# Products of the matrix of ones at seven places of TensorE's program, in an encoder of two layers

## What is computed

```
for l in range(DEPTH):                       # DEPTH = 2
    u = rms_norm(h, attn_norm_w[l])
    (dn_q, ..., ml_kr) = split_columns(u @ w_in[l])
    y_dn = gated_deltanet(...)               # 4 heads, both directions, chunked
    y_df = diff_attention(...)               # 4 heads, two softmaxes each
    y_ml = mla_attention(...)                # 4 heads, latent q and kv, rotary key
    h = h + concatenate([y_dn, y_df, y_ml]) @ w_out[l]
    u = rms_norm(h, ffn_norm_w[l])
    if l % 2 == 0: h = h + swiglu(u, w_gate, w_up, w_down)
    else:          h = h + moe_swiglu(u, router_w, ...)   # top 2 of 8 experts
return h[:, N_META:]
```

## Time and profile before

| | |
|---|---|
| median of 3 runs | 1974.53 us (1974.48 to 1975.61) |
| the profiled execution | 1975.23 us, its span 1973.4 us |
| mean granted clock of TensorE | 0.979 of full speed |
| busy: PE / DVE / ACT / POOL | 96% / 75% / 57% / 6% of the span |
| the chain that ended last | PE 88%, DVE 10%, issue 2% |
| HBM | 224 GB/s over the span |
| in-projection, first layer | about 10 to 128 us |
| mixers, first layer | 130 to 330 us |
| out-projection, feed-forward, first layer | 330 to 592 us |
| in-projection, second layer | 595 to 711 us |
| mixers, second layer | 713 to 905 us |
| out-projection, router, gather | 905 to 975 us |
| experts | 975 to 1970 us |

### The profile page before, as it was taken

How to read it: one execution, slowest core, us unless ns; L and a number is a source line. 1 busy time by engine, 2 the same in 40 slices (tenths; PEclk the granted TensorE clock), 3 DMA queues, 4 the chain that set the end, 5 groups by cost and what they waited for, 6 DMA issues and landing times.

```text
span 1973.4 us, 27118 instructions
## 1 busy us (share of the span) xinstructions
PE 1902.5 (96%) x10976; PEld 1626.6 (82%) x10976; DVE 1480.8 (75%) x1828; ACT 1125.5 (57%) x1249; POOL 117.7 (6%) x107
## 2 busy tenths in 40 slices
PE   9998989899999979999999999999999999999998
PEld 8987768899998967779888888888888888888886
DVE  8659666655549566756688888989889788888986
ACT  5644424433334633424677777677777777777775
POOL 1004131000000004140000000000000000000000
PEclk9998989999999998999899999999999999999999
DMA  7500001544453200005599999989999899999994
GB/s 298 177 28 1 1 1 68 200 171 171 155 182 134 97 28 1 1 3 180 191 364 345 353 352 366 352 333 353 358 360 347 340 358 351 358 356 364 356 361 178
DMA packets 64195, 443.56 MB, mean 225 GB/s; under 512 B 8172, under 2 KB 8204, under 8 KB 13632
## 3 DMA queue, kind: packets, MB, share of 16 engines
q1 hardware_dynamic: 62032, 437.87, 59.2%
q0 software_dynamic: 1760, 3.78, 0.5%
q10 hardware_dynamic: 272, 0.10, 0.0%
HBM read 440.66 MB, written 2.17 MB: 224 GB/s over the span
## 4 chain that ended last, share of the span: by engine, by line
PE 88%; DVE 10%; issue 2%; ACT 0%; DMA 0%; POOL 0%; SPq 0%; DVEq 0%; POOLq 0%; ACTq 0%
PE ps L1916 23%; PE ps L1918 23%; PE ps L1917 23%; PE ps L2311 2%; PE ps L2296 2%; PE ps L2315 2%; PE ps L1929 2%; DVE w_lo L1186 2%; DVE cacc L1278 2%; PE ps L2490 1%; PE ps L2090 1%; PE ps L2501 1%; PE ps L2137 1%; PE ps L2173 1%; PE ps L2102 0%
## 5 line engine op out<-in xcount | busy, mean ns | idle before, releaser
L1243 DVE TENSOR_TENSOR m_lo<-raw,m_hi 128x2048 fp32r<-128x2048 f32 x336 | 768.3, 2289 | 135.9 <-ACT m_hi L839 135.7
L839 ACT ACTIVATE m_hi<-raw 128x2048 fp32r<-128x2048 f32 x336 | 644.1, 1918 | 269.1 <-PE ps L1918 269.0
L1916 PE MATMUL ps<-m_hi,xe_hi 128*128 128x512 f32 x896 | 358.6, 400 | 0.0
L1918 PE MATMUL ps<-m_lo,xe_hi 128*128 128x512 f32 x896 | 353.6, 395 | 0.0
L1917 PE MATMUL ps<-m_hi,xe_lo 128*128 128x512 f32 x896 | 353.6, 395 | 0.0
L1186 DVE TENSOR_TENSOR w_lo<-raw,w_hi 128x1024 fp32r<-128x1024 f32 (+1 forms) x164 | 183.2, 1155 | 116.3 <-ACT w_hi L804 116.3
L1916 PE MATMUL ps<-u_hi,w_hi 128*128 128x272 f32 x800 | 236.7, 296 | 14.3 <-DVE u_lo L1236 9.9
L1918 PE MATMUL ps<-u_lo,w_hi 128*128 128x272 f32 x800 | 232.9, 291 | 0.0
L1917 PE MATMUL ps<-u_hi,w_lo 128*128 128x272 f32 x800 | 231.9, 290 | 0.0
L804 ACT ACTIVATE w_hi<-raw 128x1024 fp32r<-128x1024 f32 (+1 forms) x164 | 159.5, 1002 | 116.5 <-PE ps L1918 107.5
L1918 PEld LDWEIGHTS ps<-m_lo,xe_hi 128*128 128x128 f32 x896 | 168.0, 187 | 41.1
(11 more groups left out here) (397 smaller groups left out, 2765.4 us busy)
## 6 DMA issues: line engine op xcount, KB each, us to landing
raw<-in_moe_units SPq DMA_DIRECT2D x336, 1024.0 KB, 4.8
raw<-in_dense_units SPq DMA_DIRECT2D x57, 1024.0 KB, 4.8
raw<-in_dense_units SPq DMA_DIRECT2D x16, 768.0 KB, 5.6
raw<-in_dense_units SPq DMA_DIRECT2D x8, 896.0 KB, 4.5
w_uq<-in_mla_w_uq SPq DMA_DIRECT2D x2, 768.0 KB, 4.6
mats<-in_c_mats POOLq DMA_DIRECT2D x1, 1216.0 KB, 10.5
h<-in_h_rows SPq DMA_DIRECT2D x2, 544.0 KB, 4.4
bias_rows<-bias_row POOLq DMA_DIRECT2D x1, 1088.0 KB, 25.9
```

Source lines behind the costliest of these rows:

```text
L839: nc.scalar.activation(m_hi[k % RING][:, :], raw[:, slot, :], ACT.Copy).then_inc(m_hi_ready, 1)
L1243: V.tensor_tensor(m_lo[k % RING][:, :], raw[:, mslot(k), :], m_hi[k % RING][:, :].bitcast(F32), ALU.subtract).then_inc(m_lo_ready, 1)
L1916: mm(o, w[0], x[0], start=first, stop=False)
L1918: return mm(o, w[0], x[1], start=False, stop=last)
```

## The change

`idle_products` gets a second argument, the PSUM bank. TensorE's program calls it at seven more places. Four are in both layers:

1. behind the last `mixer_sums` of the in-projection: 9 products in bank 6;
2. before the first score of the latent attention, ahead of its two waits, with a wait of its own for `log_taken`: 9 products in bank 4;
3. before the wait for `m_prod` (s=0, d=1): 22 products in bank 4;
4. before the wait for the first level's mask of s=1, d=0, with the wait for `expcols` moved ahead of it: 10 products in bank 0.

Three are in the first layer alone: 20 products before the gate and up streams, 8 before the wait for the last hidden tile, and 11 behind the down projection. That makes 2 x 50 + 39 = 139 products. The other engines' instructions are the same as before.

```diff
-            def idle_products(n):
+            def idle_products(n, bank=6):
 
                 for _ in range(n):
-                    mm(ps[:, 6, 0:P], ones, ones, start=True, stop=True)
+                    mm(ps[:, bank, 0:P], ones, ones, start=True, stop=True)
...
                 for i in range(NORM_JOBS - 2, NORM_JOBS):
                     mixer_sums(i)
+                idle_products(9)
...
                             if t == 0:
+                                pe.wait_ge(log_taken, stat[0])
+                                idle_products(9, 4)
                                 dve_ml.wait(pe, 0, "qrot", H - 1)
                                 pe.wait_ge(rstd_used, norms_before + 3 * H)
...
                         dve_w("cols", s)
                         if d and s == 0:
+                            idle_products(22, 4)
                             dve_w("m_prod")
                         S.mark(mm(ps[:, 2 * d + 1, :], ones, flat(B[d]["TT"]), start=True, stop=True), "beta", s, d)
...
                             if n == 0:
+                                if s and d == 0:
+                                    act_w("expcols", s, d)
+                                    idle_products(10, 0)
                                 dve_w("mask", s, 0, d)
                                 act_w("expcols", s, d)
...
                     n_u[0] += KT
+                    idle_products(20)
                     for j, (gg, gu) in enumerate(zip(plan[l]["gate"], plan[l]["up"])):
...
+                    idle_products(8)
                     pe.wait_ge(hid_ready, 11)
                     residual(plan[l]["down"], (hid_hi, hid_lo), cs, T)
+                    idle_products(11)
```

## The result

The changed kernel takes 1962.76 us (median of its executions) against 1975.26 us of the kernel before, both measured again with more executions; the medians are 12.5 us apart. The ratio of the two sets of executions is 0.9923 with a 95% interval of 0.9903 to 0.9944, some 15 us less (11 to 19). The prediction said 1959.5, in 1956.5 to 1968.5.

What follows compares the result with a forecast made beforehand. PE held 88% of the chain that ended last, with ten half-clock stretches. Gains at A, C, D, E, F, H and I, less 0.2 for ten products, summed to 15.3 us off 1975.2; forecast 1959.5, range 1956.5 to 1968.5.

Steps and rivals of the forecast that it cites:

- two main scenarios: H gone and no twin: 1956.5 to 1962.5 us, chance 0.50; one fall of the pair: 1963 to 1968.5, chance 0.35.
- twin: First layer, rest at about 165 to 169 us: a fall like H ahead of PE-paced steps, losing 6.4 us.
- Price of the products: In the filled rests: 0.25 us a product, mostly covered; each group costs its excess over the wait, 0 to 0.3 us.
- Do they hold the clock: In the filled rests: products of ones raised the clock at the program's start, so they hold it; slower had chance 0.03.
- D, E, F: Half-clock stretches at 380.09, 520.04 and 595.13 us, in streams of 272 columns: give back 1.9, 1.5 and 1.5 us.
- A: Half-clock stretch at 130.92 us, first layer, between L2194 and the second beta product: gives back 1.6 us.
- B and G: Half-clock stretches at 154.81 and 735.08 us, behind beta, where TensorE waits for VectorE and POOL: give back 0.
- H: Half-clock stretch at 752.15 us, second layer, no product in its rest: 6.4 us gained if the fall is missed.
- C: Half-clock stretch at 260.63 us, with L2296 the only long PE work: gives back 1.0 us, between 0 and 1.9.
- I: Half-clock stretch at 834.07 us, PE solid for 3.41 us at half pace: gives back 1.6 us.
- first rival: H stays or its twin appears: one fall loses 6.4 us, 1966, chance 0.35; both 1972, chance 0.07.
- J: Half-clock stretch at 953.53 us, with no product: 0, up to 1.7 us either way.

Runs made afterwards that it cites:

- e7: The changed kernel with products in the remaining mixer and router rests too, and four for ten at s=1 of the second layer; 1956.68 us, ratio 0.9895.
- e3: The changed kernel without the 22 products at the beta step, in both layers; 1967.38 us, ratio 0.9958.
- e6: The changed kernel plus 7 products in the second rest (1.6 us) of the second level of s=0, both layers; 1965.18 us, ratio 0.9948.
- e10: e7 without the 22 products at the beta step, in both layers; 1955.66 us, ratio 0.9879.
- e2: The kernel before with only the 22 products at the beta step added, in both layers; 1973.05 us, ratio 0.9970.
- e11: e7 without the 8 and 7 products in the two rests of the second level of s=0, both layers; 1962.42 us, ratio 0.9919.
- e4: The changed kernel plus 8 products in the first rest (2.2 us) of the second level of s=0, both layers; 1972.92 us, ratio 0.9962.

## Why the prediction was right, and where its steps were off

The time, the sign and the range held. The point was 3.3 us low: the median lies between the prediction's two main scenarios (up to 1962.5 without a twin, from 1963 with one fall). Which of the two the traced executions were is known, 1970.3 and 1968.4 with the twin; which the 14 lower ones were is not. By its steps, on the trace of the changed kernel:

- **Price of the products**: right. 44 matmuls in 5.08 us and 40 in 4.63 are 0.115 and 0.116 us each, 20 in 2.50 are 0.125. The waits left behind them are 0.3 to 0.9 us, and 1.4 before the first layer's first latent score; the prediction had under 0.6.
- **Do they hold the clock**: yes, but for one fall in the traces, that of e7 at 837, which began as the four did. Away from the added products e7 has one more of 3.41 us, 14.6 us into the program.
- **D, E, F**: 1.9, 1.5 and 1.5 us predicted. From the first stream's start to the next, 519.96 - 382.52 = 137.44 us before (the start times are those of the matmuls behind the rests in the earlier trace rows) are 524.72 - 389.18 = 135.54; the next 75.18 are 73.68; the last, to the mixers' start, 117.94 are 116.50. That is 1.9, 1.5 and 1.4.
- **A**: 1.6 us predicted, 0.15 got: 156.35 - 131.16 = 25.19 us against 25.34 in the earlier trace rows. The second layer lost: 740.08 - 714.90 = 25.18 against 23.72. This is the step that failed. It took the second layer's full-clock time for what a cured first layer would do, and no rest inside that stretch was looked at. Half clock at 141 and at 725 us took 1.5 us in either layer. The rest before it is 1.0 us, and many of the matmuls around are small. Of the six traces of kernels that have the nine products behind the in-projection and leave this dip open (the changed kernel twice, e3 to e6), five show a fall there in at least one layer, seven falls in twelve passages in all; e3's shows none and needs 23.70 and 23.75 us. e7, which fills the dip, has 23.6 us in both layers. So A's gain is there when the dip is missed.
- **B and G**: 0 predicted. 15.17 and 15.41 us against 15.08 and 15.12; e10 bears it out for the whole kernel once the later rests are filled. With those rests open the 22 products went with 3 us (e2) and 4.6 us (e3) between medians, which the steps behind beta do not show. The prediction read VectorE's busy share as the sign that it is the bound, and that alone is no proof: D has VectorE busy in 6.75 of 6.83 us and gave back its 1.9. The Trainium skill, "TensorE: Matmul & The Clock Gate", section Terms, prices throttled time at half its length. E, F and H come near it, with 1.5, 1.4 and 6.4 us where half is 1.7, 1.7 and 6.8; D with 1.9 where half is 3.4, the twin with 6.6 where half is 10.2, and B and G with nothing do not.
- **C**: 1.0 predicted, between 0 and 1.9. From the first level to L2318 281.36 - 268.78 = 12.58 us against 12.95: 0.4, since the clock fell again during L2303, at 277.7, by the way the prediction gave as the lower end.
- **I**: 1.6 predicted and 1.6 got (9.57 us to 7.98 from L2172's start to the row sums).
- **The ten products of the second layer**: 0.2 predicted, within 0 to 1.4, and 0.7 measured from the score before them to L2318 (10.52 to 11.20 us). The step that was mis-sized is that POOL's wait would absorb the delay; POOL waited for VectorE, VectorE for PE.
- **H**: missed, as forecast, in the second layer of this execution; its steps take 8.65 us. The twin came instead. The prediction's first rival put both on one price of 6.4 us and gave one of the two 0.35; e11 shows 6 us, and 5 of 19 executions lie that far up. The reason that the prediction gave for H's absence was poor, though. It named the rest at L2102 (1.57 us). At full clock there is another 2.2 us rest ahead of it, which B had hidden in the first layer and G had cut to 1.30 us in the second, and by e4 and e6 it seems that whether the first or the second is met decides what the fall costs.
- **The sum for this execution**: -4.8 (D, E, F) - 0.15 (A) + 1.5 (the new stretch of the second layer) + 0.4 (B, G) + 6.6 (twin) - 0.4 (C) - 6.4 (H) - 1.6 (I) + 0.7 (ten) = -4.2. J, which was set at 0, gave 1.3: from the first gather to the slots' products 961.85 - 953.74 = 8.1 us against 966.98 - 957.56 = 9.4. That is -5.5. The first stream starts 0.5 us later in this execution, ahead of every edit (13.22 against 12.72), which makes -5.0, against 1970.29 - 1975.23 = -4.9. The experts' stream begins 5.1 us earlier and the span ends 4.9 earlier, so it is as long as before, as predicted.
- For the median, 1962.8: without the twin 1970.3 becomes 1963.7. That the two new stretches stand in most executions is inferred from the few traces there are, not counted. The three executions at 1974 to 1975.2 are as high as e4's traced one (1975.19), which has both falls; that they have both too is not shown.

What stays open: why e3 is so often slow, what makes five of 20 executions of the kernel before 8 to 18 us longer, and why the dips at 141 and 725 us, which the kernel before has too, were not met in its trace. The Trainium skill, "TensorE: Matmul & The Clock Gate", Part 1, says that what watches TensorE does not start afresh with a kernel. Two groups of executions of one kernel, as in e11, agree with that; the nearly equal stretches in the two traces of the changed kernel (165.0 and 163.3, 724.8 and 723.0) do not ask for it.

## What to carry to other kernels

Look at what sets the pace behind a half-clock stretch before pricing it: B's and G's 20 us of it were free here, and 13.65 us cost 6. Ask what each stretch's next paced step waits for, not which engine is busy. Filling a rest can move the fall to the next rest (e2, e4), so fill them in order up to the work that TensorE paces, or leave the chain alone; filling the first rest of a pair left the median 8 us higher than filling the second. Size a group by the wait that the trace of the new kernel shows, since a kernel at full clock has rests that the slow one hid, and too many products, or products met by a low clock, delay what follows.

## What was not expected of the hardware

PE being busy does not by itself say how soon the clock is back. At the streams' beginnings it was back after 3.41 us (E, F) or 6.83 (D, 2.4 us of it rest). In the DeltaNet levels it stayed low for 13.65 us with PE busy in all 13.65, in H and in both stretches of e4, and in 13.43 of 13.65 in that of e11; in the twin it stayed low for 20.48 us with 19.85 busy. Yet in e6 two falls ahead of the same levels lasted 3.41 us each. And a fall can be a shelter, as I read the trace: at 748.71 in the changed kernel it began early, kept PE busy through the following rest, and was over at 755.54, just as the paced steps began.
